# The tiles of the operand buffers a and b 2064 bytes apart instead of 2048, in a one-core Trainium2 kernel for two transformer-like blocks

## The chip, the cores and the metric

One core of one Trainium2 chip runs the whole program. The metric is the device time of one execution in microseconds, lower is better; the figure for a kernel is the median over several executions. TensorE multiplies a stationary 128x128 operand with a moving one of up to 512 columns, VectorE (DVE), ScalarE (ACT) and GpSimd (POOL) do the elementwise work, SyncE (SP) issues most DMAs.

## The reference

The sequence has 512 positions and 1024 channels, in float32. A first block (gated convolution, a chunked recurrence, stick-breaking attention, an MLP of width 4096) is followed by two layers of a second block (SwiGLU of width 2816, a mixer, SwiGLU again). Most of the work is products of the activations with weights:

```python
def swiglu(x, w_gate, w_up, w_down):
    return (jax.nn.silu(x @ w_gate) * (x @ w_up)) @ w_down
...
    x = x + g2 * (jnp.square(jax.nn.relu(h2 @ mlp_w1[l])) @ mlp_w2[l])
...
    proj = h @ w_in[l] + b_in[l]
...
    x = x + merged @ w_out[l]
```

## The kernel before, in words

Activations lie transposed: channels over the 128 partitions, positions along the partition. An operand of a product is eight tiles of 128 channels by 512 positions (`KT = 8`, `S = 512`), 2048 bytes per partition and tile. Every float32 product is made of three matmuls in the faster float32r format. An operand is split in a rounded high part and the low rest, and `mm3` (line 683) issues low weights by high x, high weights by low x, high weights by high x (lines 685, 686, 687), all added in PSUM.

Four buffers hold the split activations: `a_hi`, `a_lo`, `b_hi`, `b_lo` (lines 240 and 241), each `[128, 8, 512]`. They are declared right after `raw`, `w_hi` and `w_lo`, three slots of 1024 elements each (lines 236 to 238). Allocation goes in order of declaration, each tensor rounded up to 32 bytes. The first of them, `raw`, starts at byte 1152 of the partition, so `w_hi` is at 13440, `w_lo` at 25728, `a_hi` at 38016, `a_lo` at 54400, `b_hi` at 70784, `b_lo` at 87168, `xres` at 103552, and `arena`, the last and largest, at 138912. All tiles of a and b, all halves of them (256 positions, 1024 bytes) and all 128-column slices of weights in `w_hi` and `w_lo` therefore start at a multiple of 64 bytes (128 modulo 512). `q11_hi`, `t_hi`, `q11_lo` and `t_lo` (lines 263 to 265) are overlaid on the arena and hold tiles of 256 positions that are the operands of the fast products. They start at 147104, 151200, 167584 and 171680, each 32 bytes past a multiple of 64; their tiles are 1024 bytes apart, so all of them start at such an address.

Weights come as units of 128x1024 on SP's queue into `raw`; ACT rounds them to `w_hi`, POOL subtracts (`low`, line 627, instruction at line 631) into `w_lo`, PE uses them. The activations' high parts are rounded by ACT (or by DVE at lines 2790 and 3140), the low parts made by DVE (`low_part`, line 2420; `raw_low`, line 2455; lines 3005, 3085 and 3142).

Who reads a and b on TensorE: `project` (line 713), `project_fresh`, `project_merged`, `project_half` (line 755), `down` (line 770) and the last product of `mlp_chunk` and `fast_chunk` stream whole tiles of 512. `fast_product` (line 1160) streams halves of 256: of b (`b_1a`, `b_2a`, `b_2b`) in the MLP, of q11 (`x_1a`) and a (`x_2a`, `x_2b`) in the SwiGLUs, of t in both. `values_4` and `values_2` (lines 824 and 839) use slices of a as the stationary operand.

In attention of the second block, line 1369 multiplies `q_h` and `k_h`, plain float32 in two passes. Their place alternates from one pair of heads to the next (lines 367 to 370): areas from 175808, a multiple of 64, and from 163488, 32 bytes past one; inside an area the tiles lie 2048 apart.

The first block's depthwise convolution on DVE (line 2563) reads 512 elements that start one element, 4 bytes, further on with each of its taps.

Two other uses take a part of a buffer as one flat run. `b_rows` (line 334) is the first 2048 elements of b_hi and b_lo, cut by `SB_AT` and `SB_W` into pieces for stick-breaking attention (`sb_split`). `fourth` (line 467) is 1024 elements from tile 4 of a_hi and a_lo, and serves as a fourth slot for a unit of weights, once (lines 661, 1137 and 1864). The order of the work on each engine is written out by hand and tied by semaphores.

Of the kernel before, what the change touches and what calls it, by code (L numbers as in the profile page):

```python
# [22 lines left out]
F32R = mybir.dt.float32r  # L23
# [5 lines left out]
P = 128  # L29
S = 512  # L30
D = 1024
KT = D // P
TT = S // P
RING = 3
QUAD = P // 4

WIDE = 4
# [62 lines left out]
class Count:  # L100
# [19 lines left out]
    def quarter(self, more):  # L120

        value = 16 * ((self.n + more) // RING + 1)
        for register, per in self.turns:
            value = register * (16 * per // RING) + value
        return value
# [100 lines left out]
def build(nc, x_t, c_row, par1, par2, lru, forget, mod_w, first, stream, cum_rows, out_t):  # L226
    with ExitStack() as ctx:
        def sb(name, shape, dt=F32):
            return ctx.enter_context(nc.sbuf_tensor(name, shape, dt))

        def sem(name):
            return ctx.enter_context(nc.semaphore(name))


        ps = ctx.enter_context(nc.psum_tensor("ps", [P, 8, S], F32))
        raw = sb("raw", [P, RING, D])
        w_hi = sb("w_hi", [P, RING, D], F32R)
        w_lo = sb("w_lo", [P, RING, D], F32R)

        a_hi, a_lo = sb("a_hi", [P, KT, S], F32R), sb("a_lo", [P, KT, S], F32R)  # L240
        b_hi, b_lo = sb("b_hi", [P, KT, S], F32R), sb("b_lo", [P, KT, S], F32R)
        xres = sb("xres", [P, KT, S])
        params = sb("params", [P, max(N_PAR1, N_PAR2)])
        cols = sb("cols", [P, 128])
        forget_w, forget_sum = sb("forget_w", [P, KT, QUAD]), sb("forget_sum", [P, QUAD])
        ident = sb("ident", [P, P])
# [84 lines left out]

        neg_tri_made = tt[:, 0, 0:P]
        sb_out, sb_sp = hg_k, hg_g[:, 0, :]
        b_rows = [t[:, 0:4, :].rearrange("p k s -> p (k s)") for t in (b_hi, b_lo)]
        sb_split = [[[t[:, SB_AT[j]:SB_AT[j] + SB_W[j]] for t in b_rows] for j in range(TT)]]
        behind = [0, *(SB_AT[j] + sum(SB_W[1:]) for j in range(1, TT))]
        sb_split.append([[t[:, behind[j]:behind[j] + SB_W[j]] for t in b_rows] if j else [sq_hi, sq_lo] for j in range(TT)])
# [61 lines left out]
        late_loaded = [sem(f"late_loaded{i}") for i in range(2)]  # L399
        raw_loaded = [sem(f"raw_loaded{i}") for i in range(RING)]  # L400
        mod_used, mod_ready, c_ready, consts_ready = sem("mod_used"), sem("mod_ready"), sem("c_ready"), sem("consts_ready")
# [62 lines left out]

        FAST_BANK = (None, 0, 0, 2, 0)
        LAST_BANKS = (3, 2)
        fourth = [v[:, 4:6, :].rearrange("p k s -> p (k s)") for v in (a_hi, a_lo)]

        half_inverse = {0: ps[:, 7, left], TOK: ps[:, 6, right]}

# [96 lines left out]
        def _(pool):  # L567
# [34 lines left out]
            pool.drain()  # L602
            pool.tensor_tensor(forget_sum[:, :], ident[:, 0:QUAD], ident[:, QUAD:2 * QUAD], ALU.add)
            for q in range(2, 4):
                pool.drain()
                pool.tensor_tensor(forget_sum[:, :], forget_sum[:, :], ident[:, q * QUAD:(q + 1) * QUAD], ALU.add)
            pool.drain()
# [72 lines left out]
        def _(pe):  # L680
# [26 lines left out]
            def tile(last):  # L707
                last.then_inc(tiles_done, 1)
                c.tiles.n += 1
# [637 lines left out]
            def forget_quarters():  # L1347

                bank = bank_v()
                for k in range(KT):  # L1350
                    rows = slice(k % 4 * QUAD, k % 4 * QUAD + QUAD)
                    last = pe.matmul(ps[rows, bank, :], forget_w[:, k, :], xres[:, k, :], start=k < 4, stop=k >= 4, skip_group_check=True)
                tile(last)

            def forget_total():

                bank = bank_v()
                pe.wait_ge(dve_evacuated, quads_read)
                tile(pe.matmul(ps[0:QUAD, bank, :], forget_sum[:, :], f_quads, start=True, stop=True))

# [2220 lines left out]
```

## Time and profile before

| what | us |
|---|---|
| median of 3 executions (lowest, highest) | 3311.78 (3311.02, 3311.94) |
| span of the profiled execution, first to last instruction | 3309.8 |
| PE busy in it | 3294.3 |
| POOL busy in it | 2194.1 |
| DVE busy in it | 2267.4 |
| ACT busy in it | 1533.1 |

For the profiled execution only its span is given. The median stands 2.0 us above it. The granted TensorE clock was 1.000 of full speed (2.4 GHz) over the span. The records of matmuls overlap, since the engine is pipelined: one of 512 columns is listed with some 0.39 us, but the next one starts long before that. The distance from one start to the next is what a matmul costs where the engine never waits, and it is read from the timeline as the difference of two start times divided by the count between them.

### The profile page before, as it was taken

What the parts mean: (1) busy time and instruction counts of PE and PEld (TensorE: products, weight loads), DVE (VectorE), ACT (ScalarE), POOL (GpSimd) and SP (SyncE); (2) the same over time, 40 slices, a digit from 0 to 9 for tenths busy, and PEclk for the clock granted to TensorE, in tenths of its full rate; (3) what the DMA queues carried; (4) which work ended last, traced back from release to release, by engine and by line L of the source; (5) the groups of instructions that cost most, each with busy time, mean ns of one, the idle gap of its engine ahead of it and who ended that gap; (6) DMA issues with size and microseconds to landing.
All of it is one profiled execution on the core that took longest, in us unless ns stands there. A gap on an engine that the chain in (4) does not pass through costs nothing.

```text
span 3309.8 us, 54409 instructions
## 1 busy us (share of the span) xinstructions
PE 3294.3 (100%) x18310; PEld 2817.0 (85%) x18310; DVE 2267.4 (69%) x3503; ACT 1533.1 (46%) x2141; POOL 2194.1 (66%) x2139
## 2 busy tenths in 40 slices
PE   9999999999999999999999999999999999999999
PEld 5888778899889997888888999889987888888998
DVE  8887685888877778714435887777878334247877
ACT  4365664434443336735634333533347445534333
POOL 6443445877778886553356988688875543468886
PEclk9999999999999999999999999999999999999999
DMA  5221453322232223332223322233223222223232
GB/s 224 89 71 64 166 183 111 123 101 98 86 110 96 101 91 105 98 121 69 73 89 105 115 101 101 81 110 114 94 84 114 90 102 71 83 96 108 102 111 98
DMA packets 94488, 343.40 MB, mean 104 GB/s; under 512 B 10609, under 2 KB 11249, under 8 KB 93954
## 3 DMA queue, kind: packets, MB, share of 16 engines
q1 hardware_dynamic: 86978, 312.11, 26.8%
q10 hardware_dynamic: 7360, 29.29, 2.7%
q8 instruction: 94, 1.54, 0.2%
q14 instruction: 56, 0.46, 0.0%
HBM read 335.03 MB, written 2.13 MB: 102 GB/s over the span
## 4 chain that ended last, share of the span: by engine, by line
PE 87%; DVE 5%; DVEq 4%; issue 1%; ACT 1%; DMA 1%; ACTq 0%; SPq 0%
PE ps L685 26%; PE ps L687 26%; PE ps L686 26%; DVEq L2561 2%; PE ps L852 1%; PE ps L853 1%; PE ps L854 1%; PE ps L1387 1%; PE ps L1369 1%; PE ps L934 1%; DMA arena<-in_mod_w 1%; DVE arena L2761 1%; PE ps L1378 1%; DVEq L2783 0%; PE ps L793 0%
## 5 line engine op out<-in xcount | busy, mean ns | idle before, releaser
L631 POOL TENSOR_TENSOR w_lo<-raw,w_hi 128x256 fp32r<-128x256 f32 (+1 forms) x1468 | 1306.3, 921 | 907.9 <-ACT w_hi L1475 905.5
L685 PE MATMUL ps<-a_hi,w_lo 128*128 128x512 f32 (+1 forms) x2728 | 1021.0, 374 | 0.8 <-DVE a_lo L2424 0.3
L687 PE MATMUL ps<-a_hi,w_hi 128*128 128x512 f32 (+1 forms) x2728 | 1006.8, 369 | 0.0
L686 PE MATMUL ps<-a_lo,w_hi 128*128 128x512 f32 (+1 forms) x2728 | 1006.7, 369 | 0.0
L631 POOL TENSOR_TENSOR w_lo<-arena,w_hi 128x512 fp32r<-128x512 f32 x514 | 775.1, 1533 | 180.0 <-ACT w_hi L2074 119.8
L685 PEld LDWEIGHTS ps<-a_hi,w_lo 128*128 128x128 f32 x2728 | 514.1, 188 | 100.5 <-issue 17.1
L687 PEld LDWEIGHTS ps<-a_hi,w_hi 128*128 128x128 f32 x2728 | 514.1, 188 | 87.8
L686 PEld LDWEIGHTS ps<-a_lo,w_hi 128*128 128x128 f32 x2728 | 514.6, 189 | 80.8 <-issue 0.5
L1475 ACT ACTIVATE w_hi<-raw 128x1024 fp32r<-128x1024 f32 x321 | 336.6, 1053 | 323.9 <-PE ps L687 304.8
L685 PE MATMUL ps<-b_hi,w_lo 128*128 128x512 f32 (+1 forms) x1052 | 390.0, 371 | 0.6 <-POOL w_lo L631 0.2
L2074 ACT ACTIVATE w_hi<-arena 128x1024 fp32r<-128x1024 f32 x192 | 203.7, 1061 | 402.3 <-PE ps L687 402.3
L686 PE MATMUL ps<-b_lo,w_hi 128*128 128x512 f32 (+1 forms) x1052 | 387.8, 369 | 0.0
L687 PE MATMUL ps<-b_hi,w_hi 128*128 128x512 f32 (+1 forms) x1052 | 387.8, 369 | 0.0
L687 PE MATMUL ps<-t_hi,w_hi 128*128 128x256 f32 x1232 | 346.2, 281 | 0.0
L685 PE MATMUL ps<-t_hi,w_lo 128*128 128x256 f32 x1232 | 345.6, 281 | 0.0
L686 PE MATMUL ps<-t_lo,w_hi 128*128 128x256 f32 x1232 | 342.7, 278 | 0.0
L685 PEld LDWEIGHTS ps<-t_hi,w_lo 128*128 128x128 f32 x1232 | 231.9, 188 | 0.1
L686 PEld LDWEIGHTS ps<-t_lo,w_hi 128*128 128x128 f32 x1232 | 231.9, 188 | 0.0
L687 PEld LDWEIGHTS ps<-t_hi,w_hi 128*128 128x128 f32 x1232 | 231.2, 188 | 0.0
L685 PEld LDWEIGHTS ps<-b_hi,w_lo 128*128 128x128 f32 x1052 | 198.1, 188 | 37.8 <-issue 3.7
L687 PEld LDWEIGHTS ps<-b_hi,w_hi 128*128 128x128 f32 x1052 | 198.2, 188 | 33.5
L686 PEld LDWEIGHTS ps<-b_lo,w_hi 128*128 128x128 f32 x1052 | 198.2, 188 | 32.9
(365 smaller groups left out, 4977.3 us busy)
## 6 DMA issues: line engine op xcount, KB each, us to landing
raw<-in_stream SPq DMA_DIRECT2D x419, 512.0 KB, 3.2
arena<-in_stream SPq DMA_DIRECT2D x148, 512.0 KB, 3.4
arena<-in_mod_w ACTq DMA_DIRECT2D x32, 512.0 KB, 3.9
arena<-in_mod_w SPq DMA_DIRECT2D x16, 512.0 KB, 11.5
arena<-arena ACTq DMA_DIRECT2D x16, 256.0 KB, 3.7
arena<-cum_rows ACTq DMA_DIRECT2D x2, 2048.0 KB, 9.8
xres<-in_x_t SPq DMA_DIRECT2D x4, 512.0 KB, 5.3
arena<-in_first SPq DMA_DIRECT2D x8, 256.0 KB, 11.8
```

The source lines that it names most:

```text
L631: last = pool.tensor_tensor(to[:, at], of[:, at], hi[:, at].bitcast(F32), ALU.subtract)
L685: pe.matmul(out, lo, x_hi, start=start, stop=False)
L686: pe.matmul(out, hi, x_lo, start=False, stop=False)
L687: return pe.matmul(out, hi, x_hi, start=False, stop=stop)
L852: pe.matmul(out, a_hi[:, f, tok], w_lo[:, s, w], start=f == 0, stop=False)
L853: pe.matmul(out, a_lo[:, f, tok], w_hi[:, s, w], start=False, stop=False)
L854: last = pe.matmul(out, a_hi[:, f, tok], w_hi[:, s, w], start=False, stop=f == KT - 1)
L934: last = pe.matmul(ps[:, bank, t], ke[:, t], qe[:, t], start=True, stop=True)
L1369: pe.matmul(ps[:, 4 + c.sc.n % 2, w], q_h[g % 2][:, i, r * P:r * P + P], k_h[g % 2][:, i, w], start=True, stop=True).then_inc(scores_done, 1)
L1475: act.activation(w_hi[:, slot, :], raw[:, slot, :], ACT.Copy).then_inc(hi_ready, 1)
L2074: act.activation(w_hi[:, slot, :], fast_units(c.part.n)[j], ACT.Copy).then_inc(fast_hi, 1)
L2561: dve.drain()
```

## The change

A tile of a_hi, a_lo, b_hi and b_lo starts 516 elements (2064 bytes) after the one before it, instead of 512; the last four are not used. The buffers are now declared flat, the tiles are a view of them, and the two flat uses take their elements from the flat buffers: `b_rows` the first 2048 as before, `fourth` 1024 from the start of tile 4. Each buffer grows by 128 bytes, so `a_hi` starts where it did, `a_lo` 128, `b_hi` 256, `b_lo` 384 and everything declared later 512 bytes further on. No instruction is added, removed or moved.

```diff
+STRIDE = S + 4
...
-        a_hi, a_lo = sb("a_hi", [P, KT, S], F32R), sb("a_lo", [P, KT, S], F32R)
-        b_hi, b_lo = sb("b_hi", [P, KT, S], F32R), sb("b_lo", [P, KT, S], F32R)
+        operands = [sb(name, [P, KT * STRIDE], F32R) for name in ("a_hi", "a_lo", "b_hi", "b_lo")]
+        a_hi, a_lo, b_hi, b_lo = (t[:, :].rearrange("p (k s) -> p k s", s=STRIDE)[:, :, 0:S] for t in operands)
...
-        b_rows = [t[:, 0:4, :].rearrange("p k s -> p (k s)") for t in (b_hi, b_lo)]
+        b_rows = [t[:, 0:4 * S] for t in operands[2:4]]
...
-        fourth = [v[:, 4:6, :].rearrange("p k s -> p (k s)") for v in (a_hi, a_lo)]
+        fourth = [t[:, 4 * STRIDE:4 * STRIDE + D] for t in operands[0:2]]
```

## Rows read from the trace of the kernel before

**Rows 1.** The page: busy time by engine, and the chain that ended last.
```profile
PE 3294.3 (100%) x18310; PEld 2817.0 (85%) x18310; DVE 2267.4 (69%) x3503; ACT 1533.1 (46%) x2141; POOL 2194.1 (66%) x2139
PE 87%; DVE 5%; DVEq 4%; issue 1%; ACT 1%; DMA 1%; ACTq 0%; SPq 0%
```

**Rows 2.** Stretches: from, to, us; busy us of PE, PEld, DVE, ACT, POOL; clock; DMA.
```profile
642.00:900.00 258.00, 258.00 (x1619) 233.96 (x1618) 217.08 (x287) 104.25 (x138) 201.11 (x141) 1.00 0.26 94
1860.00:2450.00 590.00, 589.73 (x3850) 540.40 (x3850) 461.44 (x686) 226.32 (x273) 490.14 (x380) 1.00 0.28 100
```

**Rows 3.** Groups of PE by line: count, busy us, mean ns, idle before.
```profile
L685 PE MATMUL ps<-a_hi,w_lo 128*128 128x512 f32 (+1 forms) x2728 | 1021.0, 374 | 0.8 <-DVE a_lo L2424 0.3
L685 PE MATMUL ps<-b_hi,w_lo 128*128 128x512 f32 (+1 forms) x1052 | 390.0, 371 | 0.6 <-POOL w_lo L631 0.2 <-DVE b_lo L2889 0.2
```

**Rows 4.** Timeline of PE, 512-column products of a: start us, length us, instruction.
```profile
1905.22 0.39 PE L685 MATMUL ps<-a_hi,w_lo 128*128 128x512 f32 x1
...
1914.52 0.39 PE L687 MATMUL ps<-a_hi,w_hi 128*128 128x512 f32 x1
1914.74 0.28 PE L685 MATMUL ps<-q_hi,w_lo 128*128 128x256 f32 x1
```

**Rows 5.** Timeline of PE in the MLP: halves of b, then t tiles.
```profile
820.17 0.28 PE L685 MATMUL ps<-b_hi,w_lo 128*128 128x256 f32 x1
...
822.33 0.28 PE L685 MATMUL ps<-b_hi,w_lo 128*128 128x256 f32 x1
...
823.04 0.28 PE L685 MATMUL ps<-t_hi,w_lo 128*128 128x256 f32 x1
823.16 0.28 PE L686 MATMUL ps<-t_lo,w_hi 128*128 128x256 f32 x1
823.28 0.28 PE L687 MATMUL ps<-t_hi,w_hi 128*128 128x256 f32 x1
...
827.99 0.28 PE L685 MATMUL ps<-t_hi,w_lo 128*128 128x256 f32 x1
```

**Rows 6.** Timeline of PE in a SwiGLU: q11 tiles, then halves of a.
```profile
1914.86 0.28 PE L686 MATMUL ps<-q_lo,w_hi 128*128 128x256 f32 x1
...
1916.15 0.28 PE L685 MATMUL ps<-a_hi,w_lo 128*128 128x256 f32 x1
...
1916.50 0.28 PE L685 MATMUL ps<-a_hi,w_lo 128*128 128x256 f32 x1
...
1917.58 0.28 PE L685 MATMUL ps<-t_hi,w_lo 128*128 128x256 f32 x1
```

**Rows 7.** Line 1369, durations ns min/median/max: 1480 to 1515, then 1530 to 1565 us.
```profile
L1369 PEld LDWEIGHTS ps<-arena x16: 187/188/188, 1486.7 to 1514.5; 128*128 128x128 f32 x16
L1369 PE MATMUL ps<-arena x16: 271/431/591, 1487.0 to 1514.9; 128*128 128x128 f32 x4, 128*128 128x256 f32 x4, 128*128 128x384 f32 x4, 128*128 128x512 f32 x4
...
L1369 PEld LDWEIGHTS ps<-arena x16: 187/190/193, 1532.9 to 1560.7; 128*128 128x128 f32 x16
L1369 PE MATMUL ps<-arena x16: 272/432/595, 1533.2 to 1561.1; 128*128 128x128 f32 x4, 128*128 128x256 f32 x4, 128*128 128x384 f32 x4, 128*128 128x512 f32 x4
```

**Rows 8.** DVE, durations ns min/median/max: line 2563 (shifted starts), line 2825 (tile starts).
```profile
L2563 DVE SCALAR_TENSOR_TENSOR ps<-arena,params,ps x116: 747/753/758, 48.7 to 148.0; 128x512 f32<-128x512 f32 x116
...
L2825 DVE SCALAR_TENSOR_TENSOR xres<-ps,cols,xres x135: 733/740/752, 545.1 to 916.3; 128x512 f32<-128x512 f32 x135
```

## The prediction

> **What bounds the kernel now.** The page comes first: PE is busy for 3294.3 us of the span, 100%, and 87% of the chain that ended last is PE [rows 1]. The busy time in stretches says that this isn't an average over unlike parts: 258.00 us of 258 in the MLP's fast loop, 589.73 of 590 in a stretch with two SwiGLUs, with POOL, the next engine, at 201.11 and 490.14 us [rows 2]. The groups by line show PE idle for 0.8 and 0.6 us in all ahead of the first products of a and b [rows 3]. The clock column is 1.00, so 2.4 GHz throughout [rows 2]. So no wait sets the end; the distance between two matmuls does, and an edit that shifts addresses can only act through what one instruction takes. For that I went to the timeline of PE, and divided start times by the count of matmuls between them:
> - 512 columns of a: 42 matmuls from 1905.22 to 1914.74, 9.52 us, 226.7 ns each [rows 4]. 512 columns at 2.4 GHz are 213.3 ns, so 13.3 ns are on top.
> - 256 columns of b: 18 from 820.17 to 822.33, 120.0 ns each; of a: 9 from 1916.50 to 1917.58, 120.0 ns each [rows 5, 6]. 256 columns are 106.7 ns; again 13.3 on top. The surplus belongs to the matmul, not to its columns.
> - 256 columns of t: 42 from 823.04 to 827.99, 117.9 ns each; of q11: 11 from 1914.86 to 1916.15, 117.3 ns each [rows 5, 6]. The surplus is 11.2 and 10.6 ns.
>
> The last item matters. The same instruction with the same weights costs 2.1 to 2.7 ns less when its moving tile is t or q11. What differs is the place: all tiles and halves of a and b start at a multiple of 64 bytes, all of t and q11 32 bytes past one. Spacing inside the buffers doesn't order them (t's steps are 4096 bytes, q11's 1024, b's 2048).
>
> **The change part by part.** It adds and removes no instruction, DMA or wait; no queue is reordered. Left is where each operand starts.
>
> *The moving tiles on PE.* The three product lines stream a 2728 times and b 1052 times each [rows 3]: 3 x 3780 = 11340 matmuls. New starts: the buffers' own shifts of 128, 256 and 384 bytes keep them at a multiple of 64, and tile k lies 16k further. Tiles 0 and 4 stay at a multiple of 64; 2 and 6 come 32 past one, like t and q11; 1, 3, 5 and 7 come 16 or 48 past one, where no operand of PE in this trace starts. How often each tile is read follows from the code. The last product of the 13 MLP and 32 SwiGLU fast chunks reads only a's tiles 0 and 1: 45 x 48 = 2160. The SwiGLU fast halves read a's tiles 4 to 7: 32 x 48 = 1536. The MLP's fast halves read b's tiles 0 to 3 156 times and 4 to 7 312 times. `down` outside the loops has 15 x 48 = 720, 240 on tiles 0 and 1, 480 on 2 and 3. The remaining 6456 spread evenly, 807 a tile. In sum tiles 0 and 1: 2046 each (1080 + 39 + 120 + 807); 2 and 3: 1086 each (39 + 240 + 807); 4 to 7: 1269 each (384 + 78 + 807). Unchanged class (0, 4): 3315; class of t (2, 6): 2355; new class (odd): 5670.
>
> Price of the class of t: between -2.7 and -2.1 ns; I take -2.2, near the longer count (t, 42 matmuls), and use it at 512 columns too, as the surplus there is the same 13.3. Price of the new class, which no row shows: from below by the whole surplus, -13.3 ns; from above by the only row in which a place costs PE something. Line 1369 multiplies q_h and k_h from two areas. Where both start at a multiple of 64 its longest matmul takes 591 ns and a load at most 188; where both start 32 past one, 595 and 193 [rows 7]. That is +4 ns. The nearest rows in kind (same format, same line, same weights) are t and q11, so I take -2.2 for the odd tiles too: what I assume is that any start off a multiple of 64 helps alike.
>
> Sum: (2355 + 5670) x 2.2 ns = 17.7 us less.
>
> *Does it reach the end?* PE hasn't a gap to speak of in the stretches [rows 2], so each ns saved between starts ends up in the span while the operands keep coming. The cover is POOL's: 490.14 of 590 us busy [rows 2], 17% of slack against 0.5% asked for. Taken whole.
>
> *Stationary use.* `values_2` and `values_4` take slices of a as the stationary operand, 1056 in all, and `fourth` 16. At the same ±2 to 4 ns they are worth under 4 us either way, and I count nothing; both ends stay in the range.
>
> *DVE and ACT,* which write and read a and b at the new starts: nothing. The convolution's 116 taps read from starts that move by 4 bytes each time and take 747 to 758 ns, next to 733 to 752 for the same kind of instruction from tile starts [rows 8]. Were it otherwise, their idle time covers it (217.08 and 104.25 us busy of 258 [rows 2]); without that cover, 64 low parts in the loops at 10 ns are 0.6 us.
>
> *Flat runs.* `b_rows` and `fourth` keep order and size and start at a multiple of 64 (4 x 2064 = 8256): nothing. Arena, xres and constants move by 512 bytes, a multiple of 64: nothing, so t and q11 remain as priced.
>
> The profiled span, 3309.8, less 17.7 is 3292.1; the median stands 2.0 us above the span, hence 3294.1 us.
>
> **A rule weighed.** Rows first: 226.7 ns from start to start at 512 columns [rows 4]. The Trainium skill, page "TensorE: Matmul & The Clock Gate", section "Wait — 56ns, not 53.3ns?", has 215.7 ns for a warm matmul of that size in bf16. By it there would be 2.5 ns on top, too little for a place to matter, and the sum would be nothing; the trace disagrees by 11 ns for this format.
>
> **The rivals.**
> *Nothing measurable.* Either only tiles 2 and 6 gain, 2355 x 2.2 = 5.2 us, 3306.6, or the odd ones give back what the others gain, or t is cheaper for another reason than its start (for instance the 20480 bytes between its high and low part, against 16384 in a and b) and nothing moves: 3311.8. For it: the surplus is an even 13.3 in both widths and in every stretch, and half of the tiles go where nothing is known. Against it: t and q11 lie differently from each other and both are cheaper than b. The Trainium skill, page "SBUF — State Buffer", sections "Door 1" and "Who interferes with whom", speaks for this rival: lines of SBUF are 16 bytes, which a shift by multiples of 16 doesn't cut differently, and PE never waits for another's port. By it the time stays at 3311.8.
>
> *Slower.* One mechanism: a moving tile that starts off a multiple of 32 bytes needs a fetch more than before at its ends, and PE, which is already at its limit, pays it per matmul. Place: all 5670 matmuls of odd tiles. Price: the +4 ns of rows 7, 22.7 us, less 5.2 on tiles 2 and 6: +17.5, 3329.3. It decides from about 0.9 ns per odd tile on, where it has eaten the gain of tiles 2 and 6. For it: rows 7 say that places can cost. Against: what costs there is a start at 32, that is cheaper in rows 5, so the sign isn't that of the place alone.
>
> *Much faster.* The surplus is two reads of PE, weights and moving tile, falling on each other because both start alike, and a shift of 16 bytes already parts them. Then up to 13.3 x 8025 = 107 us go: 3205. For it: weights and a and b are alike modulo 512. Against: t and q11 are parted by 32 and keep 11 of the 13.3.
>
> **How the numbers follow.** Forecast (any start off 64 helps, 3294.1): 0.37. Much faster: 0.05. Nothing measurable: 0.31. Slower: 0.27. Within 0.2% (6.6 us) is about what a measurement of this kernel can tell from no change. A little of the nothing case (a gain of 5.2 and something for stationary use) lies past that bound: faster 0.43, same 0.31, slower 0.26. The forecast's own range is 3311.8 less 8025 x 2.7 = 21.7, less 4 for stationary use, so 3286, up to 3300. The whole range runs from 3282 to 3332: it takes in the nothing case and the slower one at its price with some us on top, and leaves out the much faster one and a dearer odd tile.
>
> **What would show it.** Right: in the timeline of the changed kernel, groups of three matmuls (one k) at 353 or so instead of 360 ns in the halves of a and b, and some 673 instead of 680 at 512 columns, for all k but 0 and 4; t and q11 as before; idle time of PE unchanged. Only k 2 and 6 shorter: the nothing case. Odd k longer than 680 ns: the slower case. It is wrong altogether if the distances stay at 226.7 and 120.0 and the time still moves, through DVE, ACT or POOL instructions whose durations changed, or if other places (arena, xres) turn out to matter although they moved by 512 bytes.

## The result and the profile after

The changed kernel takes 3328.74 us (3328.64 to 3328.98, 3 executions) against 3311.78: 1.0052 times the time before, 95% interval 1.0032 to 1.0071, so slower by 17.0 us. The time lies inside the range, on the other side of the forecast. The span of its profiled execution is 3326.9 us, 17.1 more than before.

The page of the changed kernel, busy time by engine and the chain, against [rows 1] (lines of the code are one further on than before: the three products are 686, 687, 688):
```profile
PE 3315.1 (100%) x18310; PEld 2805.8 (84%) x18310; DVE 2269.5 (68%) x3503; ACT 1533.3 (46%) x2141; POOL 2190.4 (66%) x2139
PE 93%; DVE 3%; DVEq 1%; ACT 1%; issue 1%; ACTq 0%; DMA 0%; POOL 0%; SPq 0%
```
PE gains 20.8 us of busy time, with the same 18310 matmuls; DVE, ACT and POOL are within 4 us of before. The groups of the first product, against [rows 3]:
```profile
L686 PE MATMUL ps<-a_hi,w_lo 128*128 128x512 f32 (+1 forms) x2728 | 1026.4, 376 | 0.0
L686 PE MATMUL ps<-b_hi,w_lo 128*128 128x512 f32 (+1 forms) x1052 | 392.4, 373 | 0.4 <-DVE b_lo L2890 0.2
```
Idle time ahead of them is 0.0 and 0.4 us. And the stretches, with the columns of [rows 2]:
```profile
642.00:900.00 258.00, 258.00 (x1635) 232.64 (x1634) 215.97 (x287) 105.32 (x139) 201.36 (x139) 1.00 0.28 98
1860.00:2450.00 590.00, 590.00 (x3882) 538.24 (x3881) 462.10 (x683) 225.07 (x273) 494.08 (x380) 1.00 0.29 99
```
PE has no gap, the clock is 1.00. So no new wait took the time; it must be in the distance between matmuls. The timeline of PE over one product of 24 matmuls from b, tiles 0 to 7 (start us, length us, instruction; the row after the last is the first of the next product):
```profile
2160.71 0.39 PE L686 MATMUL ps<-b_hi,w_lo 128*128 128x512 f32 x1
2160.93 0.40 PE L687 MATMUL ps<-b_lo,w_hi 128*128 128x512 f32 x1
...
2166.28 0.39 PE L686 MATMUL ps<-a_hi,w_lo 128*128 128x512 f32 x1
```
5.57 us for 24, 232.1 ns each. Before it was 226.7, on two tiles in turn [rows 4] and on eight (table below). The last product of a fast chunk reads tiles 0 and 1 alone, 36 matmuls:
```profile
1917.65 0.39 PE L686 MATMUL ps<-a_hi,w_lo 128*128 128x512 f32 x1
...
1925.93 0.28 PE L686 MATMUL ps<-q_hi,w_lo 128*128 128x256 f32 x1
...
1928.74 0.28 PE L686 MATMUL ps<-t_hi,w_lo 128*128 128x256 f32 x1
...
1931.90 0.28 PE L686 MATMUL ps<-t_hi,w_lo 128*128 128x256 f32 x1
```
From 1917.65 to 1925.93 that is 230.0 ns. The 27 matmuls of t from 1928.74 to 1931.90 take 117.0 ns each (the first of them 124, then 116.7), where 117.9 stood in [rows 5], though t moved by 512 bytes only.

Summing the distances from one matmul's start to the next over the whole trace, by kind of operand, gives a ledger. All ledgers below are made so; "halves" are the 256-column parts of a and b, "values" the matmuls with a as the stationary operand:
```
kind                    count   before us   change us
a, b at 512 columns      9167      2109.7      +29.8
halves, 256 columns      2196       265.5       -4.6
t, q11, 256 columns      4464       528.1       -6.4
values                   1056       139.6       -1.0
other matmuls            1426       260.9       -0.6
sum                                            +17.2
```
The sum is the 17.1 us of the span, as it must be: distances hold PE's waits too. The medians over unbroken series of matmuls say what one costs:
```
kind                                   before ns   after ns
512 columns, tiles 0 to 7 in turn         226.67     231.96
512 columns, six on two tiles             226.67     230.00
halves of a                               119.67     117.92
halves of b                               119.50     116.92
t                                         117.83     116.67
q11                                       117.33     116.67
```
In the ledger the 154 products of 24 matmuls carry 16.9 us of the 29.8 and the 479 of six 9.1, somewhat less than 19.6 and 9.6 us, their counts times the medians' 5.29 and 3.33 ns; products over four tiles make most of the rest. The 512-column distances up to 245 ns rose by 3.8 ns in the mean, which would be 34.9 us; the longer ones, which hold the waits, lost 5 us (25.5 to 20.4 in excess of the others). So at 512 columns the change costs, and at 256 columns it gains.

### The profile page after: what moved, and what is told of

It reads as the page before. It is cut to its first block, busy times and chain, and to the rows that moved or that the text cites. A ratio compares the mean times of both kernels' runs of the same rounds, so it can differ in the third digit from the quotient of the medians.

```text
span 3326.9 us, 54409 instructions
## 1 busy us (share of the span) xinstructions
PE 3315.1 (100%) x18310; PEld 2805.8 (84%) x18310; DVE 2269.5 (68%) x3503; ACT 1533.3 (46%) x2141; POOL 2190.4 (66%) x2139
## 4 chain that ended last, share of the span: by engine, by line
PE 93%; DVE 3%; DVEq 1%; ACT 1%; issue 1%; ACTq 0%; DMA 0%; POOL 0%; SPq 0%
PE ps L686 27%; PE ps L687 27%; PE ps L688 27%; PE ps L853 1%; PE ps L854 1%; PE ps L855 1%; PE ps L1388 1%; PE ps L1370 1%; PE ps L935 1%; PE ps L881 1%; DVE arena L2762 1%; PE ps L1379 1%; DVEq L2784 0%; PE ps L794 0%; DVE arena L2786 0%
```

## The experiments

### First: starts alone, and the change taken apart

**m1_starts** runs only PE, in a program of its own with nothing beside it: products of 72 matmuls, 3 per tile as in the kernel, each product with other byte offsets of the moving tiles (`hi`, `lo`), the step between them, and the weights (`w`), counted from a common level modulo 512.
```diff
+run(mm, hi=0), run(mm, hi=16), run(mm, hi=32), ... run(mm, hi=256)
+run(mm, step=2064, lo=128)              # the changed kernel's places
+run(mm, w=32), run(mm, w=32, hi=32), ...
```


> No part of the blocks is computed: TensorE alone streams the three float32r matmuls of a product, 72 per setting, with the start of the moving tiles and of the weights varied by setting, no other engine beside it. If the start of a tile sets the price (my theory now, call it START), the setting of the kernel before (all starts equal, 2048 apart) reads 226.7 ns from start to start at 512 columns, the setting of the changed kernel (2064 apart, low tiles 128 bytes off) 232 ns, and both 120 and 118 at 256 columns, with the four engines silent. If the changed kernel's cost comes from other engines' accesses beside it (rival BESIDE), both settings read the same, 226.7. If what costs is a shift against the weights (rival WEIGHTS), shifting the weights alone by 16, 32 or 64 bytes gives the same change as shifting the tiles by as much; if it is the step from one moving tile to the next (rival STEP), all settings in which hi, lo and all k start alike read 226.7, however far they are shifted, and only those with unlike starts are dearer.

Nothing else ran, and the kernel's distances were there. Timeline of PE; in each pair the two starts are 47 matmuls apart: everything level, tiles 32 bytes on, the changed kernel's places, weights 32 on, both 32 on.
```profile
42.80 0.39 PE L64 MATMUL ps<-x_hi,w_lo 128*128 128x512 f32 x1
...
53.45 0.39 PE L64 MATMUL ps<-x_hi,w_hi 128*128 128x512 f32 x1
...
75.96 0.39 PE L66 MATMUL ps<-x_hi,w_lo 128*128 128x512 f32 x1
...
86.93 0.40 PE L66 MATMUL ps<-x_hi,w_hi 128*128 128x512 f32 x1
...
352.01 0.39 PE L87 MATMUL ps<-x_hi,w_lo 128*128 128x512 f32 x1
...
362.91 0.40 PE L87 MATMUL ps<-x_hi,w_hi 128*128 128x512 f32 x1
...
468.22 0.40 PE L94 MATMUL ps<-x_hi,w_lo 128*128 128x512 f32 x1
...
479.19 0.39 PE L94 MATMUL ps<-x_hi,w_hi 128*128 128x512 f32 x1
...
534.73 0.39 PE L98 MATMUL ps<-x_hi,w_lo 128*128 128x512 f32 x1
...
545.39 0.40 PE L98 MATMUL ps<-x_hi,w_hi 128*128 128x512 f32 x1
```
226.6, 233.4, 231.9, 233.4 and 226.8 ns. With the other offsets of this run and the next one that used 512 columns (each a mean over 47 distances, after the first 24; one execution of each program):
```
tiles on by     0      4      8      16     32     48     64     80     96     112    128
ns            226.7  238.0  232.7  231.6  233.3  233.4  228.8  231.2  233.4  231.3  233.4
tiles on by   144    160    176    192    208    224    240    256    320    512
ns            233.3  234.3  233.4  233.3  234.7  233.4  226.7  226.7  228.9  226.7
weights on by 16: 226.7   32: 233.4   64: 233.4   128: 232.2   256: 226.7
weights and tiles on by 32: 226.7   by 64: 226.7
low tiles alone on by 16: 231.9   64: 232.0   128: 231.1   256: 226.7
low weights alone on by 64: 231.2   128: 231.1
step 2064: 232.1   2080: 232.6   2112: 231.6   2176: 232.3   2304: 226.7
```
Three things follow. No other engine is needed. It isn't the tile's own start: a tile that lies 32 bytes on is as cheap as before once the weights lie 32 on as well, and weights that move alone cost as much. And 256 bytes on is no move at all, for tiles, low tiles, weights or the step. What counts is the start of the moving tile against the start of the weights, modulo 256. Level is the cheapest that was found; of the other places only 240 (and weights on by 16, which is the same thing) reaches it. One pair departs a little from the relation: weights on by 128 read 232.2 and tiles on by 128 read 233.4, although both are 128 apart.

**e1_shift_only** is the changed kernel with the step back at 2048 bytes: tiles of a_hi and b_hi stay level with the weights, those of a_lo and b_lo lie 128 off.
```diff
-STRIDE = S + 4
+STRIDE = S
-        operands = [sb(name, [P, KT * STRIDE], F32R) ...
+        operands = [sb(name, [P, KT * STRIDE + 32], F32R) ...
```


> Tiles 2048 bytes apart as before, buffers 128 bytes longer, so that low tiles start 128 bytes off the high ones and the rest moves by 512 as in the changed kernel. If the 16 bytes from tile to tile cost (STRIDE), this is as before, 3311.8, with 226.7 ns at 512 columns, perhaps 5 us less from t and q11. If the 128 bytes between high and low cost (DISTANCE), this carries the whole of it: 3328.7 and about 232 ns.

3333.42 us, 1.0067 [1.0054, 1.0079], +21.5: more than the whole change, without its step. The step of 2064 isn't needed for the loss. Timeline of PE, a product of 24 from b:
```profile
2163.14 0.40 PE L686 MATMUL ps<-b_hi,w_lo 128*128 128x512 f32 x1
...
2168.74 0.40 PE L686 MATMUL ps<-a_hi,w_lo 128*128 128x512 f32 x1
```
5.60 us, 233.3 ns each; the ledger has +33.3 us on a and b at 512 columns.

**e2_stride_only** keeps the step of 2064 and makes the buffers 256 bytes longer than before, so that the high and the low tile k start alike modulo 256.
```diff
-        operands = [sb(name, [P, KT * STRIDE], F32R) ...
+        operands = [sb(name, [P, KT * STRIDE + 32], F32R) ...
```


> Tiles 2064 bytes apart, each buffer 256 bytes longer than eight tiles of 2048, so that high and low tiles of the same k are alike modulo 256 again. STRIDE: 3328.7 as the changed kernel, with groups of three at 686 to 708 ns by k. DISTANCE: 3311.8 and 680. If both add, each of the two kernels shows a part of the 17 us.

3334.37 us, 1.0068 [1.0056, 1.0080], +22.5, ledger +34.8 on a and b at 512. Each half of the change costs more by itself than both together, and they don't add. That they don't add fits m1, where one offset costs 4.4 (low tiles 128 on) or 5.4 ns (step 2064) and both together 5.2. But e1 is dearer than m1 says: of its 128 products of 24 without a longer distance than 245 ns, 47 stand at m1's 231.1 and 62 at 233.3 ns. The same offsets have more than one price, which comes back below.

### Second: does the relation hold in the kernel

**m2_starts** adds settings to m1: finer and odd offsets, weights that step along with the tiles, other widths.
```diff
+run(mm, hi=4), run(mm, hi=240), run(mm, hi=512), run(mm, n=384), run(mm, n=128), ...
+run(mm, step=2064, wstep=528)
```


> No part of the blocks is computed: TensorE alone streams the three float32r matmuls of a product, as in the first kernel of this kind, with further settings. The theory so far (RELATIVE): the price hangs on the start of the moving tile less the start of the weights, modulo 256 bytes. It expects tiles shifted by 512 as by 0 (226.7 ns at 512 columns) and tiles shifted by 320 as by 64 (113.3 ns at 256 columns); weights stepping by 528 with tiles stepping by 2064 as nothing shifted (226.7), and weights stepping by 528 alone as dear as tiles stepping by 2064 alone (232). A rival (LOW BITS: only the place inside a line of 16 or 32 bytes counts) expects a shift by 4 or 8 bytes to differ from 0 and 240 to be like 16. The last groups try what stands before: if a rhythm set by the group before is kept, tiles at 32 behind tiles at 0 read 117.8 ns as in the kernel before, and 116.7 where nothing of the kind stands before.

The 512-column values are in the table above. A miss: with tiles and weights both stepping 16 bytes further (`step=2064, wstep=528`) every tile is level with its own weights, and the distance was still 230.5 ns, not 226.7. So the relation to a matmul's own weights isn't the whole rule. Nor is it that of the weights loaded beside it: the timeline shows each matmul start together with the load for the next one (both at 609.90 us, for one), and in this setting the tile is level with those weights in two of three matmuls and 240 off, which is free by itself, in the third (112 off after the last tile). Weights that step alone took 232.0, as expected. The rival LOW BITS falls with 240, which is as cheap as 0 and not like 16. 384 columns took 173.3 ns and 128 columns 111.7, level or 64 off. A second miss: at 256 columns, tiles 64 or 320 on, expected at 113.3, took 117.8 here. Tiles 64 on had taken 113.3 ns in m1, and tiles 32 on took 116.7 there and 116.7 or 117.8 here. A different product stood before each: what ran before has a say.

**e3_shift_256** is e1 with a padding of 256 bytes for each buffer instead of 128.
```diff
-        operands = [sb(name, [P, KT * STRIDE + 32], F32R) ...
+        operands = [sb(name, [P, KT * STRIDE + 64], F32R) ...
```


> Tiles 2048 bytes apart, buffers 256 bytes longer, so a_lo, b_hi, b_lo lie 256, 512 and 768 bytes further and the rest 1024. RELATIVE: all starts are as before modulo 256, so the time is as before, 3311.8 (within 2 us), with 226.7 and 120.0 ns, although more moved than in the kernel with 128, which cost 21 us. If it is any departure of the buffers from distances of 16384 that costs (rival DISTANCE), about +21 us again.

3311.26 us, 0.9999 [0.9990, 1.0008]. The buffers lie elsewhere, flat, with the views of the change; only the place modulo 256 is the old one, and nothing is left of the loss.

**e4_arena_512** is the kernel before with xres, the constants and the arena 512 bytes further on, as in the change.
```diff
+        sb("pad", [P, P])
         xres = sb("xres", [P, KT, S])
```


> Buffers a and b as in the kernel before, 512 bytes of padding behind them, so that xres, constants, q11, t and arena lie where the changed kernel has them. If the 6.4 us that t and q11 lose in the changed kernel come from their own place (PLACE), this kernel shows them: about 3305.4, t at 116.7 ns. If they come from what PE does before them, a rhythm that the even starts of a and b impose (RHYTHM), nothing moves: 3311.8, t at 117.8.

3311.46 us, 1.0000 [0.9990, 1.0009], and t stays at 117.8 ns. So t's gain in the changed kernel (117.8 to 116.7, 6.4 us with q11) doesn't come from its own move, but from a and b, which run ahead of it.

**e5_t_at_64** puts q11 and t another 32 bytes on, 64 off the weights, where m1 had shown 113.3 ns.
```diff
+            sb("pad", [P, 8])
             ARENA = 17016 - 2 * S + BRANCH
```


> Kernel before with 32 bytes of padding ahead of q11, t and arena, so that these tiles start 64 bytes off the weights modulo 256 instead of 32; a and b untouched. RELATIVE, with 113.3 ns at 64 for 256 columns: 4464 matmuls from 118.3 to about 113.4 ns, 21 us less, 3290, if POOL keeps up. If t's price is not that of its start but of its steps or of the rhythm, nothing moves: 3311.8. If starts at 64 also trouble the other readers of the arena, some us come back.

3312.84 us, 1.0004 [0.9995, 1.0013]: a clear miss. t took 117.8 ns, as tiles 64 off do in m2 behind level tiles of 256 columns (and in m3 below behind level ones of 512).

### Third: what ran before, and the weights in the kernel

**m3_rhythm** takes for each offset of 256-column tiles 168 matmuls behind 48 level ones of 512 columns.
```diff
+run(mm, hi=0, passes=2), run(mm, hi=R, n=256, passes=7)   # R = 0, 16, ... 240
```


> No part of the blocks is computed: TensorE alone, in turns 48 matmuls of 512 columns with everything alike and 168 of 256 columns whose tiles start r bytes off, r from 0 to 240, as in a fast chunk of a SwiGLU. The theory (RELATIVE with RHYTHM): what a matmul of 256 columns costs hangs on r and on the step in which the two streams of PE are left by the matmuls before. It expects 120.0 ns at r = 0, 117.8 at 32 and 64 (not the 113.3 that 64 had read behind tiles at 48), and leaves open which r, if any, reaches 113.3 behind aligned 512 columns. Without a rhythm (r alone decides), 64 reads 113.3 again here. Within 3 groups the 512 columns return to 226.7 in either theory.

The view of one line gives, for each kind, the count, the duration ns min/median/max, and the first and last start. Tiles 0, 32, 64 and 112 bytes on:
```profile
L65 PE MATMUL ps<-x_hi,w_lo x56: 278/283/283, 49.4 to 69.2; 128*128 128x256 f32 x56
...
L69 PE MATMUL ps<-x_hi,w_lo x56: 277/279/283, 111.3 to 130.6; 128*128 128x256 f32 x56
...
L73 PE MATMUL ps<-x_hi,w_lo x56: 280/280/282, 172.6 to 192.1; 128*128 128x256 f32 x56
...
L79 PE MATMUL ps<-x_hi,w_lo x56: 275/275/281, 265.5 to 284.2; 128*128 128x256 f32 x56
```
56 matmuls of every third lie 165 distances apart: 120.0, 117.0, 118.2 and 113.3 ns from these rounded starts; the unrounded ones of the same trace give 120.00, 116.67, 117.77 and 113.33. That makes a miss of the 117.8 expected at 32, and a hit of the 117.8 at 64, where "r alone decides" had 113.3. The steady distances for all offsets behind level tiles of 512 columns:
```
tiles on by      0      16     32     48     64     80     96     112
ns, 256 columns  120.0  118.7  116.7  118.3  117.8  120.0  120.0  113.3
tiles on by      128    144    160    176    192    208    224    240
ns, 256 columns  120.0  116.7  118.7  119.3  117.8  119.2  118.3  117.2
```
Each product settles within a few matmuls into a pattern that repeats, and which one depends on the offset and on what stood before: with tiles 32 on it was 116.7 directly behind level products of 512 columns, but 117.8 behind a level one of 256, the figure of t in the kernel before; behind a product with the changed kernel's halves it was 116.7, with the very pattern 113, 116, 117, 120 that t shows after the change.

**e6_weights_32** moves nothing but the weights, by 32 bytes; a, b and all behind them by 512.
```diff
+        sb("pad0", [P, 8])
         w_hi = sb("w_hi", [P, RING, D], F32R)
...
+        sb("pad1", [P, 120])
         a_hi, a_lo = ...
```


> Kernel before with the weights' buffers alone 32 bytes further; a and b 512 bytes further, tiles 2048 apart, all else 512 bytes further. RELATIVE: 512 columns at 233.3 ns instead of 226.7 (about 9167 x 6.7 ns = 61 us more), halves of a and b at 118, t and q11, which now lie level with the weights, at 120 (7 us more): about 3375. If only the tiles' own starts count (OWN START), all starts of moving tiles are as before: 3311.8.

**e7_all_32** moves a and b along with the weights, and the rest by 512.
```diff
+        sb("pad0", [P, 8])
         w_hi = sb("w_hi", [P, RING, D], F32R)
...
+        sb("pad1", [P, 120])
         xres = sb("xres", [P, KT, S])
```


> Kernel before with the weights' buffers and a and b 32 bytes further, so that they are level again; the rest 512 bytes further. RELATIVE: a and b as before, 226.7 and 120.0; t and q11 now level with the weights, 120.0 ns instead of 118.3: 3311.8 + 7.6 = 3319. OWN START: tiles at 32 past 64 cost at 512 columns what the shifted ones did, 3311.8 + 60, and the weights don't matter.

Timeline of PE, a product of 24 from b, in e6:
```profile
2212.56 0.40 PE L687 MATMUL ps<-b_hi,w_lo 128*128 128x512 f32 x1
...
2218.16 0.40 PE L687 MATMUL ps<-a_hi,w_lo 128*128 128x512 f32 x1
```
and in e7:
```profile
2188.74 0.39 PE L687 MATMUL ps<-b_hi,w_lo 128*128 128x512 f32 x1
...
2194.18 0.39 PE L687 MATMUL ps<-a_hi,w_lo 128*128 128x512 f32 x1
```
5.60 us, 233.3 ns each, against 5.44, 226.7. e6 took 3358.36 us, 1.0143 [1.0126, 1.0160], +46.9: a kernel in which no moving tile changed its place modulo 512 loses nearly three times as much as the change. e7 took 3321.75 us, 1.0031 [1.0019, 1.0042], +10.3: a and b, level again, are at their old price though they start 32 bytes past a multiple of 64, and t and q11, which moved by 512 bytes alone, are now level with the weights and at 120.0 ns instead of 117.8 and 117.3 (ledger: +8.6 us). This is the sharpest test of the relation: both signs, with neither operand's own place deciding.

e6 was 14 us cheaper than 9167 x 6.67 ns = 61 us. Its ledger has +46.9 on a and b at 512: the mean distance rose from 230.1 to 235.3, the steady one from 226.7 to 233.3. Two things make up the difference, about half each. The distances up to 245 ns were not all at 226.7 before: their mean rose by 5.9 ns (227.35 to 233.24), 54 us. The longer ones became fewer, 183 to 159, and their excess over the others fell from 25.5 to 18.5 us. That a slower PE finds its operands ready more often is the likely reading of the latter; it was not tested.

### Fourth: can it be used

**e8_fast_112** puts q11, t and the halves of a in the fast chunks of the SwiGLUs, all of 256 columns, 112 bytes off the weights, modulo 256. The MLP's halves of b stay level, and a's and b's tiles of 512 columns keep their place modulo 256; the arena lies 576 bytes further.
```diff
+        fast_hi_a, fast_lo_a = (t[:, 4 * S + 28:KT * S + 28].rearrange("p (k s) -> p k s", s=S) for t in a_flat)
...
+            q11_hi, q11_lo = (t[:, 4:4 + 4 * TOK].rearrange("p (k n) -> p k n", n=TOK) for t in t_flat)
...
-                return a_hi[:, 4 + k, 0:TOK], a_lo[:, 4 + k, 0:TOK]
+                return fast_hi_a[:, k, 0:TOK], fast_lo_a[:, k, 0:TOK]
```


> Kernel before with the 256-column operands of the fast products of the SwiGLUs (q11, t and a's tiles 4 to 7) and t of the MLP 112 bytes off the weights modulo 256, where TensorE alone read 113.3 ns behind aligned 512 columns; b and everything of 512 columns level as before. RELATIVE with RHYTHM: the SwiGLUs' 256-column matmuls go to 113.3: 1536 halves of a from 120.1 (10 us) and 3216 of t and q11 from 118.3 (16 us); the MLP's t, 1248, come behind b halves at 0 and may or may not (0 to 6 us). So 3280 to 3286, if POOL and ACT keep up with a PE that is 4% faster there. If in the kernel PE's waits between the products break the rhythm, 117 to 118 ns and about 3305.

3304.82 us against 3311.44 beside it, 0.9980 [0.9971, 0.9989]: faster by 6.6, not by 25 or more. Timeline of PE, 72 matmuls of a's halves and t in a SwiGLU:
```profile
1913.91 0.28 PE L689 MATMUL ps<-a_hi,w_lo 128*128 128x256 f32 x1
...
1922.07 0.28 PE L689 MATMUL ps<-a_hi,w_lo 128*128 128x256 f32 x1
```
8.16 us, 113.3 ns each, as wanted. Then the gain is given back. The waits of PE and its loads (us in total, times, longest), and the stretch of [rows 2]:
```profile
PE ps L689 <- POOL w_lo L635: 6.9, 29, 0.5
...
PEld ps L689 <- POOL w_lo L635: 10.7, 30, 0.6
```
```profile
1860.00:2450.00 590.00, 586.42 (x3855) 532.15 (x3854) 492.82 (x690) 227.03 (x277) 494.43 (x383) 1.00 0.29 100
```
PE now waits for the low weights from POOL, 6.9 us in 29 waits where [rows 3] had 0.2, its loads 10.7 us in 30, and its busy time falls to 586.42 of 590. In the ledger the long distances (over 150 ns at 256 columns, 245 at 512) of t, of a's halves and of a's tiles hold 18.5 us more than before, about the 18.8 us that are missing to 3286. PE, four to seven ns faster in every fast matmul, gets ahead of the low weights that POOL makes.

**e9_fast_32** moves only the halves of a's fast chunks, to 32 bytes off, where t and q11 already are.
```diff
+        fast_hi_a, fast_lo_a = (t[:, 4 * S + 8:KT * S + 8].rearrange("p (k s) -> p k s", s=S) for t in a_flat)
```


> Kernel before with a's fast halves 32 bytes further, level with t and q11, which stay where they are. RHYTHM: without halves at 0 between them the SwiGLUs' t and q11 (3216) drop from 117.8 to 116.7 though they don't move (4 us), and the 1536 halves of a go from 120.1 to 116.7 (5 us): about 3303. If a tile's price is its place's alone, t stays at 117.8 and only the halves gain: 3307.

3305.28 us, 0.9981 [0.9972, 0.9990], -6.2, close to what was expected. In the SwiGLUs the halves went from 119.67 to 116.67 ns (-3.3 us), and t and q11, not moved, from 117.8 and 117.3 to 116.67 (-3.4 us): nothing level of 256 columns runs ahead of them any more, and 116.67 is what m3 has for that order. In the MLP, where b's halves stay level, t stays at 117.9. Both versions beat both kernels, by little; e8 and e9 can't be told apart.

## Why the prediction was wrong

*What bounds the kernel: right.* PE idles for at most 0.3 us of both stretches, before and after, and DVE, ACT and POOL changed by less than 4 us. "Taken whole" was a little too much: the distances up to 245 ns at 512 columns grew by some 35 us, and 5 of them were taken back in the longer ones, so the end moved by less than the sum of the steady prices. An edit of addresses could only act through the distance between matmuls, and did.

*"I take -2.2 ... and use it at 512 columns too, as the surplus there is the same 13.3": this step failed.* It was taken from rows of 256 columns alone, and 9167 of the 11363 matmuls on a and b have 512. There the price of leaving the level has the other sign: +5.3 ns in turn over tiles 0 to 7, +3.3 on tiles 0 and 1. At 256 columns it even had the right size: -1.8 ns on halves of a, -2.6 on halves of b. An equal surplus at one place said nothing of the surplus at another.

*"Any start off a multiple of 64 helps alike": wrong in its variable.* The price goes by the offset between moving tile and weights modulo 256, not by the tile's own start. t and q11 were cheaper not for lying 32 past a multiple of 64 but for lying 32 off the weights (e7 leaves their place modulo 512 as it is, makes it level, and takes the gain away). By the same mistake tiles 0 and 4 were priced at nothing. In the changed kernel the three matmuls of tiles 0 to 7 take 687, 692, 689, 690, 699, 704, 707 and 699 ns, none of them 680. m1's product with the same places has the same eight within 1 ns (686 to 708), so nothing beside PE makes them. For tiles 0 and 4 one cause is that a_lo and b_lo lie 128 off everywhere. Another is what ran before: in e2, where high and low tile 0 are both level, it still takes 697.

*t and q11 "remain as priced": wrong,* by -6.4 us. Their own move of 512 bytes is neutral, as said (e4), but their neighbours changed.

*Moves by 512 bytes, flat runs, DVE, ACT: nothing, right* (e3, e4). Use as the stationary operand: -1.0 us, inside the 4 that were set aside.

*The rivals.* "Slower" gave 3329.3 us, and 3328.7 came; but its mechanism, a fetch more at the ends of odd tiles, is refuted: e1 has no odd tile and loses 21.5 us, e6 has none either and loses 46.9, and in the changed kernel the even tiles are dearer too. The agreement is chance, the odd tiles' +4 ns being of the size of what all tiles lost. The +4 ns itself, read in [rows 7] as the price of a place, isn't one. In the changed kernel the two areas lie where they did modulo 512, and both read alike:
```profile
L1370 PEld LDWEIGHTS ps<-arena x32: 187/188/189, 1494.3 to 1568.3; 128*128 128x128 f32 x32
L1370 PE MATMUL ps<-arena x32: 270/431/592, 1494.6 to 1568.7; 128*128 128x128 f32 x8, 128*128 128x256 f32 x8, 128*128 128x384 f32 x8, 128*128 128x512 f32 x8
```
No 595 and no 193 is left. e4, which moves the same areas by 512 bytes and leaves a and b, still has 595. What changed around them is where a and b start, so this price too was not that of the areas' own place. "Much faster" named the right relation, weights against moving tile, and had its sign wrong for 512 columns: level is the cheapest there, and to be parted is what costs. "Nothing measurable" leaned on two statements of the Trainium skill, page "SBUF — State Buffer", sections "Door 1" and "Who interferes with whom". The runs disagree with what was made of them: a shift by a multiple of 16 bytes isn't free. The Trainium skill, page "TensorE: Matmul & The Clock Gate", section "Step-by-step: what each phase is for", has two independent read ports of PE, so that loading the next weights takes nothing from the running matmul. By that, weights that move alone would change nothing; they cost 6.7 ns a matmul in m1 (226.7 to 233.4) and 46.9 us in e6.

*What is not settled.* That the two reads get in each other's way in SBUF is the nearest reading of a price that hangs on their distance, but no run shows the conflict itself. A rule that gives the figures isn't there: why 240 off is as cheap as 0 and 16 off is not, why weights on by 128 aren't the same as tiles on by 128, why tiles and weights that step together cost 230.5, and which pattern a product falls into behind which other.

*What a reader could have done before.* The rows held a warning: t and q11, both 32 off, cost 117.9 and 117.3 [rows 5, 6], so the place alone didn't fix the price even at one width. The transfer to 512 columns, with 81% of the matmuls on a and b, deserved both signs.

## What to carry to other kernels

Where PE is the bound and float32r matmuls follow each other without a gap, keep the starts of the moving tiles level with the starts of the weights modulo 256 bytes for 512 columns, padding in steps of 256 bytes; a pad of 16 or 128 bytes ahead of the tiles alone cost 2 to 3% of the distance in m1, and 0.7% of the kernel's time in e1 (low tiles 128 off) and e2 (16 bytes from tile to tile). For 256 columns it is worth trying to leave the level (32 or 112 bytes off, not 80, 96 or 128, which read 120.0 like 0 in m3), and to look next at who delivers the weights. A price read at one width, place and neighbourhood holds for these alone: measure it at the width that carries the sum.

## What the runs showed of the hardware that was not expected

- A float32r matmul that is level with its weights takes its columns at 2.4 GHz and 13.3 ns more, at 256, 384 and 512 columns (120.0, 173.3, 226.7 ns). Off the level, 256 columns go down to 113.3 ns, and 512 up to 238.0, the dearest, at an offset of 4 bytes, where 256 columns are dearest too (123.3).
- At 128 columns the distance is 111.7 ns, nearly that of 256; there the load of the weights, or something else that doesn't depend on the columns, seems to be the limit.
- Matmuls have a memory of what ran before: the same 256-column product took 116.7 or 117.8 ns (32 bytes off), and 113.3 or 117.8 (64 off), for as long as it was repeated, 72 to 168 matmuls.
- A slower PE won part of its loss back in fewer and shorter long distances: 7 us in e6, 5 us in the changed kernel.
